# A Hymba-style layer with a mixture of experts on one core: the second block's input rows by products instead of a gather

## The reference, cut to what matters

```
xp = xp + mix_p                      # the residual stream, here called x2
hp = rms_norm(xp, g_ffn)             # xp * rsqrt(mean(xp*xp) + eps) * g_ffn
logits = x2d @ w_router + b_router   # x2d is hp, 520 rows of 1024
top_v, top_e = lax.top_k(logits, 4)
...                                  # tokens are sorted into blocks by expert
hh = xb @ w_up[e] + b_up[e]          # xb: the rows of hp that belong to the block
ys = clamped_swiglu(hh) @ w_down[e] + b_down[e]
```

## Time and profile before

| | us |
|---|---|
| median of 3 runs | 1361.76 (1359.62 to 1363.31) |
| the profiled execution | 1363.97 |
| its span, first to last instruction | 1362.2 |
| PE busy in the span | 1296.0 (95%), 6338 MATMUL records |
| DVE / ACT / POOL busy | 918.4 / 279.6 / 123.4 |
| DMA | 468.94 MB, mean 344 GB/s over the span |
| share of the ending chain | PE 72%, DMA 20%, DVE 4%, SP's issue 2% |

### The profile page before, as it was taken

One profiled execution on the slowest core, in us unless ns is written; L12 is line 12 of the kernel. 1 busy time (PEld: TensorE's weight loads), 2 busy tenths in 40 slices (PEclk: granted clock), 3 DMA queues, 4 the chain that ended last, 5 costly groups with the idle time before them and its releaser, 6 DMA issues.

```text
span 1362.2 us, 21430 instructions
## 1 busy us (share of the span) xinstructions
PE 1296.0 (95%) x6338; PEld 525.9 (39%) x6338; DVE 918.4 (67%) x1875; ACT 279.6 (21%) x532; POOL 123.4 (9%) x227
## 2 busy tenths in 40 slices
PE   8999999988989999997999999899999997999997
PEld 6876565553323333332333332233333332333332
DVE  3215246645677878776777777587777775787788
ACT  4331133323111212111111211121121211121122
POOL 2000000000011011010101111010101100110100
PEclk9999989998989999999999999999999999999999
DMA  9405173046999999999999999999999999999995
GB/s 361 117 4 188 32 226 114 32 192 250 395 410 371 423 420 421 411 421 422 418 411 413 418 419 420 416 419 412 420 416 420 419 422 421 420 402 422 412 416 226
DMA packets 91408, 468.94 MB, mean 344 GB/s; under 512 B 11870, under 2 KB 29520, under 8 KB 41074
## 3 DMA queue, kind: packets, MB, share of 16 engines
q1 hardware_dynamic: 75070, 441.56, 79.8%
q0 software_dynamic: 7360, 16.79, 3.2%
q10 hardware_dynamic: 8948, 10.19, 2.2%
HBM read 614.82 MB, written 28.77 MB: 472 GB/s over the span
## 4 chain that ended last, share of the span: by engine, by line
PE 72%; DMA 20%; DVE 4%; SPq 2%; issue 1%; ACT 0%; DVEq 0%; POOLq 0%; POOL 0%; ACTq 0%
PE ps L1965 34%; DMA raw<-in_w_down_dram 19%; PE ps L2066 17%; PE ps L1658 5%; PE ps L1681 5%; PE ps L1905 4%; SPq L584 2%; DMA x_rows<-expert_inputs,row_idx 1%; PE ps L1852 1%; PE ps L1851 1%; PE ps L1636 1%; DVE v_gate L1597 0%; PE ps L1760 0%; PE ps L1843 0%; DVE xT L1485 0%
## 5 line engine op out<-in xcount | busy, mean ns | idle before, releaser
L1965 PE MATMUL ps<-raw,xT 128*64 128x512 f32 x2880 | 635.8, 596 | 19.6 <-DMA raw<-in_w_up_dram 16.5
L1485 DVE STREAM_TRANSPOSE xT<-x_hold 32x64 f32<-32x64 f32 (+1 forms) x688 | 276.4, 402 | 160.2 <-PE ps L1965 138.5
L1965 PEld LDWEIGHTS ps<-raw,xT 128*64 128x64 f32 x2880 | 205.8, 138 | 439.9 <-issue 402.1
L2066 PE MATMUL ps<-raw,aT 128*64 128x512 f32 x1440 | 325.9, 597 | 19.0 <-DMA raw<-in_w_down_dram 15.9
L1485 DVE STREAM_TRANSPOSE aT<-act_g 32x256 f32<-32x256 f32 x360 | 228.4, 635 | 65.3 <-PE ps L2066 53.7
L2066 PEld LDWEIGHTS ps<-raw,aT 128*64 128x64 f32 x1440 | 100.7, 137 | 237.3 <-issue 184.5
L933 ACT ACTIVATE act_s<-act_g 128x512 f32<-128x512 f32 x46 | 29.0, 630 | 649.5 <-DVE act_g L1469 649.5
L539 POOL DMA_INDIRECT slot_outputs<-y_rows,out_idx x44 | 45.2, 1028 | 620.1 <-ACT y_rows L938 619.2
L1281 DVE STREAM_TRANSPOSE bias_up<-up_cols 128x1024 f32<-128x1024 f32 x46 | 57.3, 1245 | 1.6
L1905 PE MATMUL ps<-w_out_sb,mixT 128*128 128x512 f32 x128 | 57.6, 599 | 0.8 <-DVE mixT L1218 0.8
L531 POOL DMA_INDIRECT x_rows<-expert_inputs,row_idx x48 | 50.7, 1057 | 82.6 <-DVE row_idx L1298 47.0
(11 more groups left out here) (380 smaller groups left out, 858.3 us busy)
## 6 DMA issues: line engine op xcount, KB each, us to landing
raw<-in_w_up_dram SPq DMA_DIRECT2D x360, 1024.0 KB
raw<-in_w_down_dram SPq DMA_DIRECT2D x184, 1024.0 KB, 10.5
slot_outputs<-zeros ACTq DMA_DIRECT2D x1, 8320.0 KB, 28.0
raw<-slot_outputs SPq DMA_DIRECT2D x8, 1024.0 KB, 16.1
w_c_cols<-in_w_in_dram SPq DMA_DIRECT2D x1, 4096.0 KB, 31.4
w_out_sb<-in_w_out_dram SPq DMA_DIRECT2D x1, 4096.0 KB, 13.8
w_a_cols<-in_w_in_dram SPq DMA_DIRECT2D x1, 2624.0 KB, 12.8
x_sb<-in_x_prompt_dram SPq DMA_DIRECT2D x4, 512.0 KB, 5.0
```

The costliest lines, as they stand in the source:

```text
L1485: dve.transpose(dst_at(rows_out, group), src_at(rows_in, parity)).then_inc(done, 1)
L1965: ins = mm(ps[SUB * i:SUB * i + SUB, banks[bank], :], rows_in[:, j, :], raw[:, SLOT[j], c:c + HF], start=False, stop=(j == UPU - 1), skip_ ...
L2066: ins = mm(ps[SUB * i:SUB * i + SUB, 2, :], aT[:, j, r, :], raw[:, units[j], D * r + HF * i:D * r + HF * i + HF], start=False, stop=(j == ...
```

## The change

For block 1 the gather goes. DVE makes `hit_rms`, fp32: for each tile t (rows x 64) a one where the token has that slot, times the token's factor 1/rms (now kept in `x2_rstd`). PE multiplies it with the residual rows: for each of the eight feature groups j and each tile t, `product(j)` (128 x 64) += x2(rows, every eighth column from j).T times `hit_rms`. These are 40 products: eight with 24 rows and 32 with 128. ACT copies the eight results to `xT`, scaled by `g_ffn` (new small load `g_ffn_cols`). With it go `indices(1)`, `find(1)`, `gather(1)` and the eight transposes of `turn_rows(1)`.

On PE `own_rows()` is put behind `first_up(5)`, and `first_up(6)`, `table()` and `first_up(7)` behind the order's product. `turn_rows(2)` moves behind the last unit of `second_up`, `place()` in `third_up` one unit ahead. On DVE `destinations()` moves ahead of `clamp(1)`. On SP the first two down units of block 0 are issued without the waits that stood ahead of them, block 2's loads are written out ahead of the loop, and in every block the two table words of the down units are read behind the up units.

```diff
@@ gpsimd
             def gather(b, o=None):
                 if o is None:
-                    pool.wait_ge(idx_ready, b + 1)
-                if isinstance(b, int) and b in (1, 2, 3):
-                    pool.wait_ge(x0_psum, 2 * b)
+                    pool.wait_ge(idx_ready, 2 if b else 1)
+                if isinstance(b, int) and b == 2:
+                    pool.wait_ge(x0_psum, 2)
+                elif isinstance(b, int) and b == 3:
+                    pool.wait_ge(x0_psum, 6)
...
             pool.wait_ge(h2_stored, 16 * NTILE)
-            gather(1)
             gather(2)
@@ sync
                         load_up(0, j, None)
+                    load_down(0, 0, None)
                 sp.wait_ge(h2_ready, t + 1)
...
+            load_down(0, 1, None)
+            sp.wait_ge(part_psum, NTILE)
             sp.wait_ge(h2_stored, 16 * NTILE)
             sp.wait_ge(caches_stored, 2 * 16)
-            sp.wait_ge(lg_psum, NTILE)
-            for j in range(DNU):
+            for j in range(2, DNU):
                 load_down(0, j, None)
-            sp.wait_ge(table_made, 1)
-            nb = block_count(sp)
             sp.dma_start(g_final_bc[:], ...)
-            with sp.Fori(2, nb) as b:
+
+            def load_block(b):
                 e_up, new_up = expert(sp, b), is_new(sp, b)
-                e_dn, new_dn = expert(sp, b - 1), is_new(sp, b - 1)
                 for j in range(UPU):
                     sp.wait_ge(up_used, UPU * b + (j + 1 - UPU))
                     load_up(e_up, j, new_up)
+                e_dn, new_dn = expert(sp, b - 1), is_new(sp, b - 1)
                 for j in range(DNU):
...
+            sp.wait_ge(table_made, 1)
+            load_block(2)
+            nb = block_count(sp)
+            with sp.Fori(3, nb) as b:
+                load_block(b)
@@ scalar
+                act.dma_start(g_ffn_cols[:], g_ffn[0].rearrange("(p c) -> p c", c=UPU)).then_inc(ld_small, 16)
...
+            def take_product():
+                for j in range(UPU):
+                    if j in (0, UPU // 2):
+                        act.wait_ge(x0_psum, 3 + 2 * j // UPU)
+                    act.activation(xT[:, j, :], product(j), ACT.Copy,
+                                   scale=g_ffn_cols[:, j:j + 1]).then_inc(xT_ready, 2)
...
             seed_up(1, (0, 1))
-            take_turned(1, xT)
+            take_product()
@@ vector
-            compare(shifted[:].unsqueeze(2))
+            for t in range(NTILE):
+                r = rows[t]
+                step(dve.tensor_scalar(hit_rms[0:r, t, :], slots_row[0:r, 1:SUB + 1], shifted[0:r, t:t + 1], x2_rstd[0:r, t:t + 1],
+                                       ALU.is_equal, ALU.mult))
+            settle()
+            dve.sem_inc(hit_ready, 1)
...
-            indices(1)
...
             turn_a(0, aT)
+            destinations()
             dve.wait_ge(aT_ready, 8)
             clamp(1)
...
             swiglu(own, 1)
-            destinations()
@@ tensor
             first_up(5)
-            find(1)
-            for j in range(6, UPU):
-                first_up(j)
             mark_written((0, 1))
+
+            def own_rows():
+                pe.wait_ge(hit_ready, 2)
+                for j in range(UPU):
+                    for t in range(NTILE):
+                        r = rows[t]
+                        ins = mm(product(j), t_x2[t][0:r, j:D:UPU], hit_rms[0:r, t, :], start=(t == 0),
+                                 stop=(t == NTILE - 1))
+                    if j % 4 == 3:
+                        ins.then_inc(x0_psum, 1)
+
+            own_rows()
             pe.wait_ge(order_made, 1)
             mm(ps[:, ORDER_BANK, 0:NE], ones_f[0:NE, :], blocks_ahead[:], ...).then_inc(order_psum, 1)
-            turn_rows(1)
-            pe.drain().then_inc(mixer_left, 1)
...
             def second_up():
...
-                    if j in (0, 2):
-                        pe.wait_ge(xT_ready, 24 + 4 * j)
+                    pe.wait_ge(xT_ready, 18 + 2 * j if j < 2 else 32)
...
-                    if j == 6:
+                    if j == UPU - 1:
                         turn_rows(2)
             def third_up():
...
-                    if j == 4:
+                    if j == 3:
                         place()
...
+            first_up(6)
+            table()
+            first_up(7)
+            pe.drain().then_inc(mixer_left, 1)
             pe.sem_inc(dn_used, 2 * DNU)
-            table()
             second_up()
```

More of the change, by code:

```diff
@@ L115, in moe_layer @@
         blk_row = keep("blk_row", [1, 2 * BLKS + 3], I32)
+        hit_at = keep.at
         hit = keep("hit", [P, NTILE, 2, SUB], BF16)
@@ L120, in moe_layer @@
         found = keep("found", [P, 1])
+        g_ffn_cols = keep("g_ffn_cols", [P, UPU])
         far_half = keep("far_half", [P, 1])
@@ L228, in moe_layer @@
         pidx = R("pidx", [P, 1])
+        x2_rstd = R("x2_rstd", [P, NTILE])
         before = R("before", [P, P], BF16)
@@ L251, in moe_layer @@
         gla_state = B("gla_state", [P, 9, 2, DV])
+        hit_rms = nc.alloc_sbuf_tensor_at("hit_rms", [P, NTILE, SUB], F32, offset=base + hit_at)
         chosen = nc.alloc_sbuf_tensor_at("chosen", [P, NTILE, TOPK, NE], F32, offset=base + chosen_at)
@@ L389, in moe_layer @@
         QUAD = [slice(32 * i, 32 * i + SMALL) for i in range(4)]
-        LOADED_SAMPLE, LOADED_SMALL = 5 * 16, 7 * 16
+        LOADED_SAMPLE, LOADED_SMALL = 5 * 16, 8 * 16
         def state_bank(c):
@@ L449, in turned, with product @@
             return ps[0:SUB, TURN_BANKS[b][a], :].rearrange("p (c h s) -> p h c s", c=4, h=2)[:, h]
+        def product(j):
+            return ps[:, TURN_BANKS[1][j // 4], SUB * (j % 4):SUB * (j % 4) + SUB]
         block = ctx.enter_context(nc.Block())
@@ L926, in hold @@
             def hold(b):
-                act.wait_ge(gathered, 16 * b + 16)
+                act.wait_ge(gathered, 16 * b)
                 act.wait_ge(xT_ready, 16 * b)
@@ L1238, in residual @@
                 dve.wait_ge(x2_root, t + 1)
-                do(dve.reciprocal(norm[0:r, 26:27], norm[0:r, 25:26]))
+                do(dve.reciprocal(x2_rstd[0:r, t:t + 1], norm[0:r, 25:26]))
                 if t == 0:
                     dve.wait_ge(ld_attn, 32)
-                dve.scalar_tensor_tensor(h2[0:r, :], x2[0:r, :], norm[0:r, 26:27], g_ffn_bc[0:r, :], ALU.mult,
+                dve.scalar_tensor_tensor(h2[0:r, :], x2[0:r, :], x2_rstd[0:r, t:t + 1], g_ffn_bc[0:r, :], ALU.mult,
                                          ALU.mult).then_inc(h2_ready, 1)
@@ L1292, in indices @@
             def indices(b):
-                dve.wait_ge(list_psum, b + 1)
+                dve.wait_ge(list_psum, 2 if b else 1)
                 if b:
-                    dve.wait_ge(gathered, 16 * b)
+                    dve.wait_ge(gathered, 16)
                 do(dve.tensor_reduce(found[:], ps[:, 5, 0:4], AX, ALU.add))
@@ L1954, in turn_rows @@
             def turn_rows(b):
-                pe.wait_ge(gathered, 16 * b + 16)
+                pe.wait_ge(gathered, 32 if b else 16)
                 for a in range(2):
```

## The result

The changed kernel takes 1381.38 us, the median of four runs (1380.71 to 1382.57), where the kernel before took 1362.53 in the runs beside it (1359.62 to 1364.76). The ratio is 1.0141 with a 95% interval of 1.0119 to 1.0162: some 19 us slower. The forecast was 1370.1 with a range up to 1374.0: the right sign, a size far too small.

A forecast was written before the change was run, and what follows sets the result against it. The loop was taken as bound by the weight-load DMA stream, whose start PE sets. Without a clock effect +1.2 us, a fallen clock 7.1 more: +8.3 on the median 1361.76, 1370.1 us; range 1360.5 to 1374.0.

The forecast's parts named there:

- The products: Forty products ahead of `second_up`: 10.9 us without a clock effect (8.5 to 12.0), ending at 339.7 with a fallen clock.
- The load is the bound, not the stream: In the forty products, two weight loads each, 0.11 us apart, set the time: 8.5 us for eighty.
- The clock: Falls to 1.2 GHz 4.5 us into the products; the 6.4 us left become 12.2, `second_up` 7.1 later; chance 0.50.
- The factor of 1.9 for the lower clock: Products left after the clock's fall take 1.9 times as long, 12.2 us for 6.4.
- The work behind the products: Order, `first_up(6)` 3.4 us, table 0.7, `first_up(7)` about 2.2; from products' end at 339.7 to `second_up` at 346.1.
- The start: `first_up(5)` ends at 322.53; after `mark_written`, 0.4 to 0.5 us counted, the new products begin at 323.0.
- one more small issue: `g_ffn_cols` on ACT at the program's start, beside long column products on PE; no cost named.
- From `second_up` to `place()`: Eight units with `find(2)` 14.0 us, block 2's turn 1.0, `down(0)` 6.9, four units of `third_up` 6.9.
- It goes on to the end: PE later by d from 389 us on makes the weight stream, and the end, later by d.
- the hole of the earlier trace: Gap in the weight-load stream at 425 to 430 us, 2.3 us empty, taking that much of the stream's late start.
- a held clock: Rival 1: clock stays full through the products, +1.2 us (-1.2 to +2.3), 1363.0 us; chance 0.35.
- the three rivals: Clock holds, +1.2 us (0.35); faster, hidden weight loads, -5.4 us (0.08); change off the path, about 1362 to 1364 (0.07).

The follow-up runs named there:

- contiguous: The changed kernel with each of the forty products taking 128 neighbouring columns of x2 as weights: products 16.9 us, span 5.6 us shorter than the changed kernel's 1379.2.

## Why the prediction was right and wrong

*The products* are the step that failed, by the price of a weight load. "The load is the bound, not the stream" was right. The 0.107 us for a load was taken from the earlier trace rows, whose weights lie side by side, and used for weights 32 bytes apart; the step of the operand, which stands in the diff (`j:D:UPU`), was never asked about. The load takes 0.24 at either clock, where 0.107 at full clock and 0.20 at half were counted. 16.7 us were forecast with a fallen clock, 22.0 measured: 5.3 of the missing 8.5. It also put the upper bound (12.0 without a clock effect) too low. A row with this very step did exist: the turn of `x_rows` loads 64 columns of step 8, and at the full clock eight of them took 1.02 us, 0.13 for 64 columns. Twice that for 128 would have been 0.26 us a load, 20 for eighty. Each turn also streams 128 columns, so that row couldn't prove it; as the nearest row it should have been the bound.

*The clock.* Direction and time were right: full for some four us, then 0.5 until 352, without a gap in PE's work. The reason given, the small share of the time in which the array streams, was not tested: the products under which it fell have short streams and many weight loads at once, and those under which it held (512 columns for each load) have neither. Its price was not right. The 5.8 us that it was to add to the products exist only for neighbouring columns (contiguous: 16.9 us, as forecast; at full clock eight groups of 1.40 would be 11.2, an estimate). In the changed kernel it cost what it did to the work behind. The factor of 1.9 for the lower clock was a little high: the pair in `attend` that the prediction names went from 0.42 to 0.73, which is 1.74, and the contiguous group from 1.40 to 2.51, 1.79.

*The work behind the products.* From their end to `second_up` 6.4 us were forecast and 7.9 measured, since the order's product (0.56) wasn't counted, the table took 0.98 for 0.7, `first_up(6)` 3.6 for 3.4, `first_up(7)` 2.3 for 2.2, the drain 0.42 for 0.25; with 0.15 that the forecast lost in rounding, 1.5 more.

*The start.* The products began at F + 2.41, forecast F + 2.42. F itself was 1.35 late: "one more small issue" counted on a semaphore for which PE waits, and its landing, not its issue, was the price.

*From `second_up` to `place()`* 28.8 us were forecast, 29.0 measured. Together: 8.3 + 5.3 + 1.5 + 1.35 + 0.2 = 16.7 us, against 16.8 at `place()`.

*The rest.* "It goes on to the end" was right: 16.8 at `place()`, 17.0 at the end. The credit of 2.3 us that the hole of the earlier trace rows was to take of the stream's delay came to nothing, and it stood in no term of the +8.3: the loads behind it are released by PE, and the changed kernel has a hole of its own (share 0.90 and 0.81 in the ten us from 440). SP's, DVE's and the early down loads' parts were costed at nothing, the earlier `place()` at 1.7 gained; the run with all of them and the gather allows from 1.0 us gained to 2.5 lost, so the 1.7 shows in the rows alone. *Rivals:* a held clock would have lost most of it too, as the strided load hardly feels the clock. By an estimate it gives back 0.7 us in the products (8 x 2.66 against 22.0) and 2.8 behind them (7.9 us against the 5.1 of the prediction's sum without a clock effect). None of the three rivals allowed a load dearer than the 0.11 of the earlier trace rows. Some *luck* is in how near the 16.7 us came to the contiguous products' 16.9: 10.9 for 11.2 us at full clock and a fall after 4.5 for 4.0 us make it short, 1.9 for 1.79 makes it long.

## What to carry to other kernels

Before a new product is priced, look at the access pattern of its weights, not only at its size: here fp32 columns four or eight elements apart cost 0.24 us per 128 at either clock, where neighbours cost 0.11 at the full clock and 0.21 at half. So a good access pattern pays only as far as the clock holds. If small products are bound by their weight loads, exchange the operands, so that the few columns are the weight and the many stream; and let successive products change between the array's column halves. A load added to a shared semaphore can delay everyone who waits for the sum (1.35 us here), however late its data is used.

## What the runs showed that was not expected

- The cost of a strided weight load jumps between a step of 2 and of 4 fp32 elements (0.54 to 0.89 us for the first three intervals of a group at full clock) and hardly grows to 8 (0.90).
- A load at step 8 takes 0.24 us at the full clock and at half of it.
- The clock fell 3.8 to 5.6 us into the products whether the rows alternate or not and whether the step is 1 or 8; with 512 streamed columns for each load it stayed up. Within the products PE had no gap in any of them. Which property of the short products lowers it isn't settled by these runs.
- The mixer ends within a span of 5.2 us from profile to profile, more than most of the effects studied here, and most of it goes with the time that its clock spends at the lower level (6.8 to 17.1 us).
